# A decoder layer step on one core: the first norm's modulation weights in two column halves, and one slice of modulation weights moved out of the weight ring

## The chip, the cores and the metric

The kernel runs on one NeuronCore of a Trainium2 chip, as one program. The metric is the device time of one execution in microseconds (us). TensorE (PE) does the matrix products, VectorE (DVE), ScalarE (ACT) and GpSimd (POOL) the elementwise work; SyncE (SP), ACT and POOL issue DMA transfers.

## The reference, cut to what matters

```
mod = (silu(c) @ w_ada + b_ada).reshape(B, 1, 9, 1024)      # w_ada: 1024 x 9216
sh1, sc1, g1, sh2, sc2, g2, sh3, sc3, g3 = mod[:, :, 0..8]
h = rms_norm(x, norm_ffn1) * (1 + sc1) + sh1
x = x + 0.5 * g1 * ((silu(h @ ffn1_w_gate) * (h @ ffn1_w_up)) @ ffn1_w_down)
h = rms_norm(x, norm_mix) * (1 + sc2) + sh2
...                                   # h @ w_in; block-sparse and differential attention; w_out
x = x + g2 * mixed
h = rms_norm(x, norm_ffn2) * (1 + sc3) + sh3
x = x + 0.5 * g3 * SwiGLU_2(h)
```

There are 256 prompt tokens with one conditioning vector, and 8 sample tokens with a vector each, which read a paged cache of 1024 past positions. Model width is 1024, feed-forward width 2816. All is float32.

## The kernel before

**Layout.** Activations lie feature-major: 128 partitions times KC = 8 chunks times T = 264 tokens (256 prompt, 8 sample). Each float32 product is done as three products of rounded parts: a weight block `raw` is cut by ACT into `whi` (helper `hi`, L675) and by DVE into the rest `wlo` (helper `lo`, L973); the activations are cut likewise into `hhi` and `hlo`. `product` (L1437 to L1439) multiplies whi with hhi, whi with hlo, wlo with hhi. A weight block is 1024 x 256 values (1 MB): 8 chunks of rows times two column halves t = 0, 1, so 48 products; `hi` and `lo` cut one half of the columns at a time.

**Weight ring.** SP loads the blocks in the order of `stream_plan` into four slots `raw0` to `raw3`. A load into a slot waits until the slot's former block has been used up: for a weight block until `lo` of its second half is done, for modulation weights until PE has multiplied them. `whi` and `wlo` have two buffers each, so `hi` of half t of block n waits for the products of that half of block n-2 (`s_gemm`).

**Modulation.** The 9 x 1024 columns of `w_ada` are worked in five parts of 2048 columns (`sc` = 0 to 4, the last one of 1024), each as four pairs of row blocks: `ada(sc, q, key)` (L1464) multiplies one pair (2 MB, 8 products of 512 columns, L1488). Part 0 holds sh1 and sc1, so it has to be complete before the first norm can be applied: pairs 0 and 1 go through the ring, pairs 2 and 3 into the `early` buffers, all of them ahead of the first weight block. Parts 1 and 2 are interleaved with the first feed-forward's pairs of blocks i = 0 to 7, one ring pair each. Of part 3, pairs 0 and 1 lie outside the ring (`held_ada`, loaded by POOL when the first feed-forward's up and gate products are done) and pairs 2 and 3 go through the ring behind block W_QK; all four are multiplied by PE between the down projection and the q/k projection, in `down(..., with_ada=True)`. `mod_add` (L976) transposes a part's result and adds the bias.

**The first norm.** PE transposes x (`x_turn`, L1510), DVE copies it out of PSUM (L1074), ACT squares it (L680), PE sums the squares (`norm_sum`, L1496), ACT takes the root (L685), DVE the reciprocal (L993). After `mod_add(0)` and `coefficients` DVE and ACT make hhi and hlo chunk by chunk (`norm_rows`, L1002 and L1020; `norm_hi`, L704). Gate block 0 is multiplied chunk by chunk behind them (`block_both`), up block 0 as a whole.

**A feed-forward turn** i: gate block (banks 0, 1) and up block (banks 2, 3); ACT applies Silu to the gate banks (`silu`, L710), DVE multiplies (`act_mul`), ACT and DVE cut the result (`act_hi`, `act_lo`). The next gate block waits for `s_sil`, the next up block for `s_act`. The down projection has 12 blocks (W_DN1 = 22 on), then come W_QK (34) to 37, then key, value and gate blocks among the cache's streaming: 32 uses of 2 MB each, half loaded by SP (kvA) and half by POOL (kvB), three slots each. Semaphore thresholds fix the order of all of it by hand; every engine runs its own list in order.

## Time and profile before

| | |
|---|---|
| three runs | 788.3, 791.13, 791.59 us; median 791.13 us |
| profiled execution | 791.1 us, of it 789.4 us span |
| PE busy | 733.2 us, 93% of the span |
| DVE, ACT, POOL busy | 480.1, 320.8, 121.6 us |
| HBM read and written | 205.3 and 3.2 MB, 264 GB/s over the span |

The profile lists matmuls as they go through the array: a float32 product of this size appears as two instructions for the modulation products and the sums of squares, as one for the three cut products. Times are from the span's start. "x16" is a merged run of 16 instructions; the bracket behind a row is the engine's idle time before it and what ended it.

### The profile page before, as it was taken

How to read it: one execution, taken by the hardware profiler on the slowest of the kernel's cores; microseconds unless marked ns; L12 is line 12 of the kernel's file. 1: busy time of each engine (PE TensorE's matmuls, PEld its weight loads, DVE VectorE, ACT ScalarE, POOL GpSimd, SP SyncE). 2: the span in 40 equal slices, each digit the busy share in tenths (PEclk: the TensorE clock that was granted, in tenths of full speed). 3: DMA queues.
4: the chain of work that ended last, by engine and by line, in shares of the span. 5: the costliest groups of instructions: out<-in, count | busy, mean ns of one | idle time of the engine just before them, and what ended most of it. 6: DMA issues, size and time to landing. Idle time of an engine off the chain costs nothing.

```text
span 789.4 us, 16961 instructions
## 1 busy us (share of the span) xinstructions
PE 733.2 (93%) x6610; PEld 651.9 (83%) x6610; DVE 480.1 (61%) x684; ACT 320.8 (41%) x515; POOL 121.6 (15%) x175
## 2 busy tenths in 40 slices
PE   4599999999999798988868999999989999999997
PEld 2379898999998698877855666669979999999997
DVE  1635444564444699989988644677766455464451
ACT  1434343444433453423223534455445344444431
POOL 0000000001000300867873332310000000000000
PEclk9899999999999899999988999999999999999999
DMA  8979898858754993999999999996535555646530
GB/s 352 382 262 353 294 321 292 268 171 311 258 191 164 346 340 94 341 405 403 407 403 357 402 406 354 324 370 229 168 100 161 182 191 161 204 154 200 158 111 28
DMA packets 116521, 209.53 MB, mean 265 GB/s; under 512 B 6715, under 2 KB 100187, under 8 KB 104163
## 3 DMA queue, kind: packets, MB, share of 16 engines
q1 hardware_dynamic: 107360, 163.66, 59.7%
q0 software_dynamic: 8864, 44.82, 14.8%
q8 instruction: 46, 0.75, 0.4%
q14 instruction: 25, 0.20, 0.1%
q10 hardware_dynamic: 226, 0.10, 0.0%
HBM read 205.31 MB, written 3.24 MB: 264 GB/s over the span
## 4 chain that ended last, share of the span: by engine, by line
PE 72%; DVE 13%; DMA 9%; issue 2%; ACT 2%; SPq 1%; ACTq 0%; DVEq 0%
PE bank L1437 19%; PE bank L1438 19%; PE bank L1439 19%; DMA early<-in_w_ada 3%; PE bank L1793 3%; PE bank L1488 2%; DMA kvA<-in_cache_k_moba 2%; DMA kvA_lent<-in_cache_k_moba 2%; DVE kvA L1156 2%; DVE kvB L1156 1%; PE bank L1753 1%; DMA raw<-in_w_in 1%; PE bank L1682 1%; DVE wlo L973 1%; PE bank L1754 1%
## 5 line engine op out<-in xcount | busy, mean ns | idle before, releaser
L973 DVE TENSOR_TENSOR wlo<-raw,whi 128x1024 fp32r<-128x1024 f32 (+1 forms) x177 | 209.0, 1200 | 194.7 <-ACT whi L675 191.9
L1437 PE MATMUL bank<-hhi,whi 128*128 128x264 f32 x992 | 290.5, 293 | 15.0 <-DVE wlo L973 11.1
L1438 PE MATMUL bank<-hlo,whi 128*128 128x264 f32 x992 | 285.3, 288 | 0.0
L1439 PE MATMUL bank<-hhi,wlo 128*128 128x264 f32 x992 | 284.9, 287 | 0.0
L675 ACT ACTIVATE whi<-raw 128x1024 fp32r<-128x1024 f32 (+1 forms) x192 | 194.9, 1035 | 126.1 <-PE bank L1439 86.4
L1437 PEld LDWEIGHTS bank<-hhi,whi 128*128 128x128 f32 x992 | 191.1, 193 | 28.4 <-issue 19.1
L1438 PEld LDWEIGHTS bank<-hlo,whi 128*128 128x128 f32 x992 | 191.2, 193 | 0.2
L1439 PEld LDWEIGHTS bank<-hhi,wlo 128*128 128x128 f32 x992 | 190.2, 192 | 0.0
L1437 PE MATMUL bank<-ahi,whi 128*128 128x264 f32 x416 | 119.6, 288 | 0.4 <-DVE alo L1395 0.4
L1439 PE MATMUL bank<-ahi,wlo 128*128 128x264 f32 x416 | 118.1, 284 | 0.0
L1438 PE MATMUL bank<-alo,whi 128*128 128x264 f32 x416 | 117.8, 283 | 0.0
L1437 PEld LDWEIGHTS bank<-ahi,whi 128*128 128x128 f32 x416 | 78.2, 188 | 0.9 <-DVE alo L1395 0.6
L1438 PEld LDWEIGHTS bank<-alo,whi 128*128 128x128 f32 x416 | 78.3, 188 | 0.2
L1439 PEld LDWEIGHTS bank<-ahi,wlo 128*128 128x128 f32 x416 | 78.4, 188 | 0.0
L444 POOL DMA_DIRECT2D kvB<-in_cache_k_diff x44 | 23.2, 528 | 120.7 <-issue 66.5
L710 ACT ACTIVATE sil<-bank 128x528 f32<-128x528 f32 x22 | 13.4, 611 | 61.6 <-PE bank L1439 61.6
L714 ACT ACTIVATE ahi<-act 128x528 f32 (+1 forms) x22 | 14.2, 646 | 54.2 <-DVE act L1027 54.2
L630 POOL TENSOR_TENSOR wlo<-raw,whi 128x1024 fp32r<-128x1024 f32 x15 | 35.8, 2388 | 2.8 <-issue 2.5
L444 POOL DMA_DIRECT2D kvB<-in_cache_v_diff x44 | 23.3, 529 | 49.6 <-PE bank L1793 40.9
L1753 PE MATMUL bank<-hhi,whi 128*128 128x264 f32 x96 | 28.5, 297 | 0.0
L1031 DVE TENSOR_TENSOR alo<-act,ahi 128x528 f32 (+1 forms) x22 | 15.6, 709 | 19.2 <-ACT ahi L714 19.2
L1754 PE MATMUL bank<-hlo,whi 128*128 128x264 f32 x96 | 27.2, 284 | 0.0
(246 smaller groups left out, 803.7 us busy)
## 6 DMA issues: line engine op xcount, KB each, us to landing
raw<-in_w_ada SPq DMA_DIRECT2D x24, 1024.0 KB, 7.4
raw<-in_ffn_w_gate SPq DMA_DIRECT2D x22, 1024.0 KB, 5.5
raw<-in_ffn_w_up SPq DMA_DIRECT2D x22, 1024.0 KB, 5.3
raw<-in_w_in SPq DMA_DIRECT2D x20, 1024.0 KB, 13.1
raw<-in_ffn_w_down SPq DMA_DIRECT2D x16, 1024.0 KB, 5.2
kvB<-in_cache_k_diff POOLq DMA_DIRECT2D x44, 256.0 KB, 6.2
kvA<-in_cache_k_moba SPq DMA_DIRECT2D x44, 256.0 KB, 8.3
kvA<-in_cache_v_moba SPq DMA_DIRECT2D x44, 256.0 KB, 6.6
```

The costliest lines, as they stand in the source:

```text
L444: eng.dma_start(rows_, cache[bass.ds(page, 1)].rearrange("a (j t) d -> (a j) (t d)", t=4)).then_inc(s_kv[ab][use % KVS], 16)
L630: nc.gpsimd.tensor_tensor(half_view(wlo[n % 2], key, t), half_view(raw[s], key, t), half_view(whi[n % 2], key, t).bitcast(F32), ALU.subtra ...
L675: nc.scalar.activation(half_view(whi[key[1] % 2], key, t), half_view(raw[s], key, t), ACT.Copy).then_inc(s_hi, 1)
L973: dve.tensor_tensor(half_view(wlo[key[1] % 2], key, t), half_view(raw[s], key, t), half_view(whi[key[1] % 2], key, t).bitcast(F32), ALU.su ...
L1156: dve.transpose(slot, slot).then_inc(s_kT[ab], 1)
L1437: mm(out, wh, xh, start=start, stop=False)
L1438: mm(out, wh, xl, start=False, stop=False)
L1439: return mm(out, wl, xh, start=False, stop=stop)
L1488: ins = mm(bank[32 * j:32 * j + 32, b, 0:n].rearrange("p (t a) -> p t a", a=32), csilu[:, kc, :], cols[:, :, j, :], start=(kc == 0), stop= ...
L1753: mm(out, wh, hhi[:, k, :], start=(k == 0), stop=False)
L1754: mm(out, wh, hlo[:, k, :], start=False, stop=False)
L1793: ins = mm(bank[32 * q:32 * q + 32, 4 + ab, :], wpad[half][:, q, ab, w0:w0 + 32], kv_slot(ab, use)[:, q, :], start=(half == 0 and c % 4 == ...
```

## The change

1. **Part 0 in two column halves.** `load_first(g, q)` loads, for half g, columns 512 g to 512 g + 511 of both sh1 and sc1, for row blocks 2q and 2q+1, as two transfers of 0.5 MB into buffers of their own (`first_ada`), so part 0 leaves the ring and `early` is gone. SP's order becomes: the identity (the first 128 columns of the constants, split off POOL's transfer), x, half 0, gate block 0, up block 0, half 1, then the ring. ACT's queue has `crow` ahead of `rows`.
2. **First norm in halves.** `prescaled(g)` multiplies four chunks of x by the reciprocal root without the modulation; `mod_half(g)` transposes the half's products and adds bias and gain; `half_hi(g)` makes four chunks of hhi with one activation each (scale and bias); `half_rows(g)` makes the scaled rows and hlo.
3. **First two blocks chunk by chunk, in two passes.** PE multiplies chunks 0 to 3 of gate block 0 and up block 0 (48 products), then half 1 of part 0 (`first_products(1, q)`), then chunks 4 to 7 of both blocks. The four `s_gemm` increments come with chunk 7. POOL cuts `wlo` of gate block 0, DVE that of up block 0. PE's list at the start is reordered: the lambda product ahead of `x_turn(1)`, the sums of squares among the products of half 0.
4. **Table loads.** One-value activations (Sqrt after the exponential, Silu after the cuts of up block 0) are added.
5. **Later pairs.** Parts 1 and 2 move from turns 0 to 7 to turns 2 to 9 (`ADA_FIRST` = 2).
6. **Part 3 wholly outside the ring.** `held_ada` has eight buffers (in memory that is free at that time); POOL loads all 8 MB where it loaded four; the ring carries W_QK to W_QK + 3 right behind the down projection's blocks. POOL's clearing of `qrow` waits until part 3 is multiplied.

The diff, cut to its core (indentation reduced):

```diff
 ADA_PRO = 4
-ADA_RING = 2
+HALVES = 2
+HALF = D // HALVES
 FF_ADA = 8
+ADA_FIRST = 2
 ADA_N2 = ADA_PRO + FF_ADA


 def stream_plan():
     plan = []
     ada = lambda c: [("ada", c, 0), ("ada", c, 1)]
-    for c in range(ADA_RING):
-        plan += ada(c)
     for i in range(NPAIR):
-        plan += [("w", W_FF1 + 2 * i)] + (ada(ADA_PRO + i) if i < FF_ADA else []) + [("w", W_FF1 + 2 * i + 1)]
-    plan += [("w", W_DN1 + u) for u in range(12)] + [("w", W_QK)] + ada(ADA_N2 + 2) + ada(ADA_N2 + 3)
-    plan += [("w", n) for n in range(W_QK + 1, W_DN2 + 12)]
+        paired = ADA_FIRST <= i < ADA_FIRST + FF_ADA
+        plan += [("w", W_FF1 + 2 * i)] + (ada(ADA_PRO + i - ADA_FIRST) if paired else []) + [("w", W_FF1 + 2 * i + 1)]
...
-        held_at = [hhi_at, hlo_at, sil_at, sil_at + 4 * UNIT]
+        held_at = [hhi_at, hlo_at] + [sil_at + 4 * UNIT * e for e in range(6)]
...
+        first_ada = [[place(f"first_ada0{q}", [P, 2, 2, HALF], where=r) for q in range(KC // 2)]]
+        r = [yst_at]
+        first_ada += [[place(f"first_ada1{q}", [P, 2, 2, HALF], where=r) for q in range(KC // 2)]]
...
+    def load_first(g, q):
+
+        for k in range(2):
+            kc = 2 * q + k
+            src = A["w_ada"][0][P * kc:P * kc + P, 0:2 * D].rearrange("p (s n) -> p s n", s=2)[:, :, g * HALF:g * HALF + HALF]
+            sp.dma_start(first_ada[g][q][:, k, :, :], src).then_inc(s_first[g][q], 16)
...
+    sp.dma_start(const[:, 0:P], A["consts"][:, 0:P]).then_inc(s_ident, 16)
...
+    for q in range(KC // 2):
+        load_first(0, q)
+    load_ff(gate_w[0], 0, ("w", W_FF1))
+    load_ff(up_w[0], 0, ("w", W_FF1 + 1))
+    for q in range(KC // 2):
+        load_first(1, q)
...
-        if i < FF_ADA:
-            load_pair(ADA_PRO + i)
+        if ADA_FIRST <= i < ADA_FIRST + FF_ADA:
+            load_pair(ADA_PRO + i - ADA_FIRST)
         load_ff(up_w[0], i, ("w", W_FF1 + 2 * i + 1))
...
-    load_w(W_QK)
-    load_pair(ADA_N2 + 2)
-    load_pair(ADA_N2 + 3)
-
-    for u in range(1, 4):
+    for u in range(4):
...
+    for t in range(2):
+        lo(W_FF1, t)
...
-    for e in range(2, 4):
+    for e in range(2, 8):
...
+    nc.scalar.activation(misc[:, 20:21], misc[:, 21:22], ACT.Sqrt)
...
+    def half_hi(g):
+        for c in range(4 * g, 4 * g + 4):
+            a.wait_ge(s_mod, g + 1)
+            a.wait_ge(s_pre, c + 1)
+            nc.scalar.activation(hhi[:, c, 0:TP], work[:, c, 0:TP], ACT.Identity, bias=mod[:, c, 0:1], scale=mod[:, KC + c, 0:1]).then_inc(s_hhi, 1)
+    half_hi(0)
     hi(W_FF1, 0)
     hi(W_FF1, 1)
-    norm_hi(0, 1, KC)
     hi(W_FF1 + 1, 0)
-    ff_turn(0, W_FF1, 0, 0, 0)
-    with a.Fori(1, FF_ADA - 1) as i:
-        ff_turn(i, W_FF1, 0, 1, i - 1)
-    for i in range(FF_ADA - 1, NPAIR):
+    hi(W_FF1 + 1, 1)
+    nc.scalar.activation(misc[:, 20:21], misc[:, 21:22], ACT.Silu)
+    half_hi(1)
+    hi(W_FF1 + 2, 0)
+    hi(W_FF1 + 2, 1)
+    silu(0, W_FF1, 0)
...
+    def prescaled(g):
+        v.wait_ge(s_rstd, 1)
+        for c in range(4 * g, 4 * g + 4):
+            dve.tensor_tensor(work[:, c, 0:TP], x[:, c, 0:TP], rstd[:, 0, 0:TP], ALU.mult).then_inc(s_pre, 1)
+        ws = work[:, 4 * g:4 * g + 4, TP:T]
+        ch.link(dve.tensor_tensor(ws, x[:, 4 * g:4 * g + 4, TP:T], rstd[:, 0:1, TP:T].broadcast_to([P, 4, TS]), ALU.mult))
+    def mod_half(g):
+        v.wait_ge(s_ada, 2 * g + 2)
+        turned = adaT[:, 256 * g:256 * g + 256]
+        ch.link(dve.transpose(turned, bank[:, 4 + 3 * g, 0:256]))
+        chunks = lambda ap: ap.rearrange("p (s c) m -> p s c m", s=2)[:, :, 4 * g:4 * g + 4, :]
+        b = chunks(par[:, R_BADA:R_BADA + 2 * KC].unsqueeze(2)).broadcast_to([P, 2, 4, 9])
+        ch.link(dve.tensor_tensor(chunks(mod[:, 0:2 * KC, :]), turned.rearrange("p (s t m) -> p s t m", s=2, t=4)[:, :, :, 0:9], b, ALU.add))
+        sc = mod[:, KC + 4 * g:KC + 4 * g + 4, :]
+        gain = par[:, R_N1 + 4 * g:R_N1 + 4 * g + 4].unsqueeze(2).broadcast_to([P, 4, 9])
+        dve.scalar_tensor_tensor(out=sc, in0=sc, scalar=1.0, in1=gain, op0=ALU.add, op1=ALU.mult).then_inc(s_mod, 1)
+        v.wait_ge(s_mod, g + 1)
+    def half_rows(g):
+        c0 = 4 * g
+        four = slice(c0, c0 + 4)
+        ws = work[:, four, TP:T]
+        def row(c):
+            v.wait_ge(s_hhi, c + 1)
+            dve.tensor_scalar(work[:, c, 0:TP], work[:, c, 0:TP], mod[:, KC + c, 0:1], mod[:, c, 0:1], ALU.mult, ALU.add).then_inc(s_h, 1)
+        def low(c):
+            v.wait_ge(s_h, c + 1)
+            dve.tensor_tensor(hlo[:, c, 0:TP], work[:, c, 0:TP], hhi[:, c, 0:TP].bitcast(F32), ALU.subtract).then_inc(s_hlo, 1)
+        ch.link(dve.tensor_tensor(ws, ws, mod[:, KC + c0:KC + c0 + 4, 1:9], ALU.mult))
+        ch.link(dve.tensor_tensor(ws, ws, mod[:, four, 1:9], ALU.add))
+        ch.link(dve.tensor_copy(hhi[:, four, TP:T], ws))
+        ch.link(dve.tensor_tensor(hlo[:, four, TP:T], ws, hhi[:, four, TP:T].bitcast(F32), ALU.subtract))
+        row(c0)
+        for c in range(c0, c0 + 4):
+            if c + 1 < c0 + 4:
+                row(c + 1)
+            low(c)
...
     variance(0)
-    mod_add(0)
-    v.wait_ge(s_mod, 1)
-    coefficients(0, R_N1)
-    norm_rows(0, W_FF1)
+    prescaled(0)
+    mod_half(0)
+    half_rows(0)
+    prescaled(1)
+    v.wait_ge(s_lo, half_done(W_FF1, 1))
     lo(W_FF1 + 1, 0)
-    ff_turn(0, W_FF1, 0, 0, 0, 0)
-    with v.Fori(1, 4) as i:
-        ff_turn(i, W_FF1, 0, 0, 1, i - 1)
+    lo(W_FF1 + 1, 1)
+    mod_half(1)
+    half_rows(1)
+    lo(W_FF1 + 2, 0)
+    lo(W_FF1 + 2, 1)
+    act_mul(0, W_FF1, 0)
+    lo(W_FF1 + 3, 0)
+    act_lo(0, 0)
+    ff_turn(1, W_FF1, 0, 0, 1, 0)
...
+    def first_products(g, q):
+        pe.wait_ge(s_first[g][q], 32)
+        for k in range(2):
+            kc = 2 * q + k
+            for j in range(4):
+                cols = first_ada[g][q][:, k, :, :].rearrange("p s (t j a) -> p s t j a", j=4, a=32)[:, :, :, j, :]
+                ins = mm(bank[32 * j:32 * j + 32, 4 + 3 * g, 0:256].rearrange("p (s t a) -> p s t a", s=2, t=4), csilu[:, kc, :], cols,
+                         start=(kc == 0), stop=(kc == KC - 1))
+        if q == KC // 2 - 1:
+            ins.then_inc(s_ada, 2)
...
     x_turn(1)
-    pe.wait_ge(s_par, 2)
-    mm(bank[:, 6, 0:2], C("ones"), misc[:, 2:4], start=True, stop=True).then_inc(s_lamsum, 1)
-    ada(0, 1, 1)
+    first_products(0, 0)
     pe.wait_ge(s_lamexp, 1)
-    for cb in range(4):
-        norm_sum(0, cb)
-    ada(0, 2, None)
-    ada(0, 3, None)
+    norm_sum(0, 0)
+    norm_sum(0, 1)
+    first_products(0, 1)
+    norm_sum(0, 2)
+    norm_sum(0, 3)
+    first_products(0, 2)
+    first_products(0, 3)
+    def chunk_products(b, n, parity, t, ks):
+        for k in ks:
+            ins = product(b + t, parity, k, 256, t * P, hhi[:, k, :], hlo[:, k, :], k == 0, k == KC - 1)
+        return ins
+    early_k = KC // 2
+    pe.wait_ge(s_hlo, early_k)
+    for n in (W_FF1, W_FF1 + 1):
+        for t in range(2):
+            pe.wait_ge(s_lo, half_done(n, t))
+            chunk_products(2 * (n - W_FF1), n, n % 2, t, range(early_k))
+    for q in range(KC // 2):
+        first_products(1, q)
+    for k in range(early_k, KC):
+        pe.wait_ge(s_hlo, k + 1)
+        for n in (W_FF1, W_FF1 + 1):
+            for t in range(2):
+                ins = chunk_products(2 * (n - W_FF1), n, n % 2, t, [k])
+                if k == KC - 1:
+                    ins.then_inc(s_gemm, 1)
...
-            ada(3, 2, ADA_N2 + 2)
-            ada(3, 3, ADA_N2 + 3)
+            ada(3, 2, None)
+            ada(3, 3, None)
```

## Rows read from the trace of the kernel before

**Rows 1.** The page: GB/s moved in 40 slices of 19.7 us.
```profile
GB/s 352 382 262 353 294 321 292 268 171 311 258 191 164 346 340 94 341 405 403 407 403 357 402 406 354 324 370 229 168 100 161 182 191 161 204 154 200 158 111 28
```

**Rows 2.** Timeline of PE, 12 to 84 us: start, us, engine, line, what.
```profile
12.69 0.69 PE L1510 MATMUL bank<-const,xtok 128*128 128x128 f32 x2
...
13.51 3.64 PE L1488 MATMUL bank<-raw,csilu 128*32 128x512 f32 x16
17.09 0.44 PE L1510 MATMUL bank<-const,xtok 128*128 128x128 f32 x2
...
21.35 3.83 PE L1496 MATMUL bank<-work,const 128*128 128x264 f32 x16
...
36.93 0.56 PE L1437 MATMUL bank<-hhi,whi 128*128 128x264 f32 x1 [6.75 <-DVE wlo L973]
...
55.54 1.06 PE L1488 MATMUL bank<-raw,csilu 128*32 128x512 f32 x8 [1.80 <-DMA raw<-in_w_ada]
...
68.34 1.92 PE L1488 MATMUL bank<-raw,csilu 128*32 128x512 f32 x16
...
82.00 1.92 PE L1488 MATMUL bank<-raw,csilu 128*32 128x512 f32 x16
```

**Rows 3.** Timeline of DVE and ACT, 13 to 36 us.
```profile
13.69 1.26 DVE L1074 COPY x<-bank 128x1056 f32<-128x1056 f32 x1 [1.61 <-PE bank L1511]
...
25.79 1.80 DVE L993 RECIPROCAL rstd<-rstd 128x264 f32<-128x264 f32 x1 [4.69 <-ACT rstd L685]
...
30.25 0.72 DVE L980 STREAM_TRANSPOSE adaT<-bank 128x512 f32<-128x512 f32 x1 [2.66 <-PE bank L1488]
...
32.55 1.99 ACT L675 ACTIVATE whi<-raw 128x1024 fp32r<-128x1024 f32 x2
...
34.44 0.89 ACT L704 ACTIVATE hhi<-work,mod 128x256 fp32r<-128x256 f32 x2
```

**Rows 4.** Groups by shape: count, busy us, mean ns, idle before.
```profile
L630 POOL TENSOR_TENSOR wlo<-raw,whi 128x1024 fp32r<-128x1024 f32 x15 | 35.8, 2388 | 2.8 <-issue 2.5
...
L1002 DVE SCALAR_TENSOR_TENSOR work<-x,mod,rstd 128x256 f32<-128x256 f32 x24 | 11.6, 482 | 0.2
...
L1488 PE MATMUL bank<-last_ada,csilu 128*32 128x256 f32 x64 | 3.7, 380 | 0.0
```

**Rows 5.** Timelines of POOL and of DVE around 328 us.
```profile
327.90 2.39 POOL L630 TENSOR_TENSOR wlo<-raw,whi 128x1024 fp32r<-128x1024 f32 x1
...
327.99 2.69 DVE L1169 TENSOR_TENSOR qrow<-qrep,const 128x32 f32<-128x32 f32 x4
...
360.17 0.51 DVE L1169 TENSOR_TENSOR qrow<-qrep,const 128x32 f32<-128x32 f32 x4
```

**Rows 6.** Timelines of SP, DVE, ACT and PE, 258 to 277 us.
```profile
258.58 9.77 SPq L509 DMA_DIRECT2D raw<-in_w_in  x4
...
264.95 0.49 DVE L1020 SCALAR_TENSOR_TENSOR hlo<-work,mod,hhi 128x256 fp32r<-128x256 f32 x1 [0.25 <-ACT hhi L704]
...
268.33 2.00 ACT L675 ACTIVATE whi<-raw 128x1024 fp32r<-128x1024 f32 x2 [3.48 <-DMA raw<-in_w_in]
...
269.49 1.23 DVE L973 TENSOR_TENSOR wlo<-raw,whi 128x1024 fp32r<-128x1024 f32 x1 [4.05 <-ACT whi L675]
...
270.86 0.56 PE L1437 MATMUL bank<-hhi,whi 128*128 128x264 f32 x1 [4.38 <-DVE wlo L973]
...
276.28 1.17 PE L1646 MATMUL bank<-sqb,const 128*128 128x264 f32 x4
```

**Rows 7.** Stretches: us, busy (count) of PE, PEld, DVE, ACT, POOL; PEclk, DMA share, GB/s.
```profile
34.00:35.00 1.00, 0.00 (x0) 0.00 (x0) 1.00 (x3) 1.00 (x3) 0.00 (x0) 0.58 0.87 349
...
41.00:42.00 1.00, 1.00 (x10) 1.00 (x9) 0.68 (x2) 1.00 (x2) 0.00 (x0) 1.00 0.39 124
...
187.00:200.00 13.00, 13.00 (x109) 13.00 (x108) 6.31 (x8) 5.33 (x6) 1.05 (x2) 1.00 1.03 406
...
296.00:316.00 20.00, 17.79 (x202) 16.55 (x200) 18.27 (x20) 6.30 (x12) 1.86 (x4) 0.91 0.30 94
```

More of the change, by code:

```diff
@@ L268, in build @@
         crow = place("crow", [CROWS, P], where=r)
-        early = [place(f"early{h}", [P, UNIT], where=r) for h in range(2 * (ADA_PRO - ADA_RING))]
+        first_ada = [[place(f"first_ada0{q}", [P, 2, 2, HALF], where=r) for q in range(KC // 2)]]
+        r = [yst_at]
+        first_ada += [[place(f"first_ada1{q}", [P, 2, 2, HALF], where=r) for q in range(KC // 2)]]
         r = [region]
@@ L532, in load_pair @@
                     load_ada(c // 4, c % 4, half, ("ada", c, half))
-            for i in range(NPAIR):
+            for i in range(1, NPAIR):
                 load_ff(gate_w[0], i, ("w", W_FF1 + 2 * i))
-                if i < FF_ADA:
-                    load_pair(ADA_PRO + i)
+                if ADA_FIRST <= i < ADA_FIRST + FF_ADA:
+                    load_pair(ADA_PRO + i - ADA_FIRST)
                 load_ff(up_w[0], i, ("w", W_FF1 + 2 * i + 1))
@@ L593, in _, with lo @@
             late = CW["dist"][0]
-            pool.dma_start(const[:, 0:late], A["consts"][:, 0:late]).then_inc(s_const, 16)
+            pool.dma_start(const[:, P:late], A["consts"][:, P:late]).then_inc(s_const, 16)
+            def lo(n, t):
+                key = ("w", n)
+                s = slot_of(key)
+                pool.wait_ge(s_raw[s], landed(key))
+                pool.wait_ge(s_hi, half_done(n, t))
+                if half_done(n, t) > 1:
+                    pool.wait_ge(s_lo, half_done(n, t) - 1)
+                nc.gpsimd.tensor_tensor(half_view(wlo[n % 2], key, t), half_view(raw[s], key, t), half_view(whi[n % 2], key, t).bitcast(F32),
+                                        ALU.subtract).then_inc(s_lo, 1)
+            for t in range(2):
+                lo(W_FF1, t)
             pool.wait_ge(s_sil, 1)
@@ L734, in _ @@
             row_root(0)
-            norm_hi(0, 0, 1)
+            def half_hi(g):
[4 more added lines that the diff above has]
+            half_hi(0)
             hi(W_FF1, 0)
             hi(W_FF1, 1)
-            norm_hi(0, 1, KC)
             hi(W_FF1 + 1, 0)
-            ff_turn(0, W_FF1, 0, 0, 0)
-            with a.Fori(1, FF_ADA - 1) as i:
-                ff_turn(i, W_FF1, 0, 1, i - 1)
-            for i in range(FF_ADA - 1, NPAIR):
+            hi(W_FF1 + 1, 1)
[4 more added lines that the diff above has]
+            silu(0, W_FF1, 0)
+            hi(W_FF1 + 3, 0)
+            act_hi(0, 0)
+            ff_turn(1, W_FF1, 0, 1, 0)
+            with a.Fori(ADA_FIRST, ADA_FIRST + FF_ADA - 1) as i:
+                ff_turn(i, W_FF1, 0, ADA_FIRST, i - ADA_FIRST)
+            for i in range(ADA_FIRST + FF_ADA - 1, NPAIR):
                 ff_turn(i, W_FF1, 0, i, 0)
@@ L997, in norm_rows @@
+            def norm_rows(t):
                 v.wait_ge(s_rstd, t + 1)
@@ L1014, in norm_rows @@
                         scaled(c + 1)
-                    if weights is not None and c == 1:
-                        lo(weights, 0)
-                        lo(weights, 1)
                     v.wait_ge(s_h, KC * t + c + 1)
@@ L1467, in ada @@
                 narrow = sc == ADAS - 1
-                if q == 0 and sc >= 2:
-                    pe.wait_ge(s_adaT, sc - 1)
+                if q == 0 and sc == 2:
+                    pe.wait_ge(s_mod, 1)
+                elif q == 0 and sc > 2:
+                    pe.wait_ge(s_adaT, sc - 2)
                 for half in range(2):
                     if key_c is None:
-                        e = 2 * (q - (ADA_RING if sc == 0 else 0)) + half
-                        landing, buf = ((s_early, early) if sc == 0 else (s_last, last_ada) if narrow else (s_held, held_ada))
+                        e = 2 * q + half
+                        landing, buf = (s_last, last_ada) if narrow else (s_held, held_ada)
                         pe.wait_ge(landing[e], 16)
@@ L1543, in ff_up @@
                     block_half(2, n, 1, t, hhi, hlo)
-            for i in range(NPAIR):
-                c = ADA_PRO + i
-                if 0 < i < FF_ADA:
+            for i in range(1, NPAIR):
+                c = ADA_PRO + i - ADA_FIRST
+                if ADA_FIRST <= i < ADA_FIRST + FF_ADA:
                     ada(c // 4, c % 4, c)
-                ff_gate(i, W_FF1 + 2 * i, 0, None if i else (s_hlo, lambda k: k + 1))
-                if i == 0:
-                    ada(c // 4, c % 4, c)
+                ff_gate(i, W_FF1 + 2 * i, 0)
                 ff_up(i, W_FF1 + 2 * i + 1, 0)
```

60 lines of the change are left out of this document (26 added, 34 removed).

## The prediction, written before the result was known

> **What bounds the kernel now.** I read the slices first. TensorE is busy for 93% of the span, so elsewhere than in a few places a cheaper DMA, ACT or DVE step is worth nothing; transfers run at 340 to 405 GB/s from slice 17 on (335 us), where the cache is streamed, after a slice of only 94 GB/s [rows 1]. The change touches two places, and I read the timeline of each engine there.
>
> At the start PE does its first weight product at 36.9 us [rows 2]. The chain of waits shows why: the last `early` buffer lands at 29.1 us and is multiplied until 30.2 us, then DVE turns it (30.25 us), scales a row, ACT makes a chunk of hhi and cuts block 0 (32.55 us, two halves in 1.99), DVE cuts wlo [rows 3]. PE is idle for 6.75 us and comes back at half clock: the granted clock is 0.58 in 34 to 35 us, full again in 41 to 42 us [rows 7], after 4.1 us of products. Later PE waits 1.80 us for modulation weights (55.54 us) and starts gate block 1 right behind them, at 56.6 us. From there on it is busy; a turn with a modulation pair lasts 82.00 - 68.34 = 13.66 us, of it 1.92 the pair [rows 2].
>
> The second place is the q/k projection. W_QK + 1 is issued only at 258.58 us, because its slot still holds modulation weights that PE has to multiply; ACT cuts it at 268.33 us after 3.48 us of waiting for the transfer, DVE at 269.49, and PE starts at 270.86 us after 4.38 us idle, again at half clock, until about 276.3 us [rows 6].
>
> **Part 3 outside the ring.** With no modulation weights behind it, the ring takes W_QK + 1 to + 3 as soon as the down projection's blocks are cut, around 250 us. What ends last is then no transfer. ACT makes its last hhi by 264.85 us (DVE takes it up at 264.95 [rows 6]), cuts a half in 1.0 us (1.99 for two [rows 3]) by 265.9, DVE, free since 265.44, cuts wlo in 1.23 us, and PE starts at 267.3 us instead of 270.9: 3.6 us. It is idle for under 1 us, so the clock stays full. The 24 products that took 276.28 - 270.86 = 5.4 us at half clock take 24 x 0.121 = 2.9 us; 0.121 is a turn without its pair, 11.7 us, over 96 products [rows 2]. That is 2.5 us more, and part 3 yields 6.1 us. DVE's `mod_add(3)` (1 us) and its cuts stay ahead of PE. What is late next is DVE's own list in the q/k turns, which moves up equally, as its first member waited for the same transfers. Does the gain last? In 296 to 316 us the transfers run at 94 GB/s and 0.30 share [rows 7]: all three cache slots are full and wait for the keys to be turned, so the streaming stage starts from the same state, only earlier. Bounds: 4.8 us if PE finds the clock lowered for half of that block, 7 us if the earlier weights also spare a wait in the streaming stage. I take 6.1. Its price: 4 MB more are fetched from 187 us on, where the DMA share is 1.03 already for 13 us [rows 7]; at 0.4 MB/us they need 10 us more. A down block is consumed in 5.8 us and loaded about three blocks ahead, 15 us or more, so I take nothing; uncovered it would be 1 to 3 us.
>
> **The start.** Half 0 is 4 MB and the two blocks 2 MB; at 0.42 MB/us (352 and 382 GB/s in the first slices contain the start-up [rows 1]) half 0 lands near 19 us, the blocks by 24, half 1 by 34. No later step waits for them, as follows. What remains is a chain through four engines, and I add it up.
>
> (a) The sum of squares. The first half of x is turned by 13.6 us and copied by 14.95 [rows 3]. PE has nothing but the small lambda product in between, then turns the second half. At half clock that takes 3.4 us (pairs of 0.69 against 0.44 [rows 2]), to 18.4. Before the change the rise came at about 17 us, with 3.6 us of modulation products (16 in 3.64) behind it; now products begin only at 18.4, so I put the rise at 22.2. Quarter 0 of half 0 takes 1.8 us at half clock and 0.93 at full (64 instructions for 3.7 us in the last part, of the same shape [rows 4]); the sums take 3.83 us at full clock [rows 2]. To 20.2 the quarter, two sums to 23.1, a quarter to 24.0, two sums to 25.9. Before it was 25.2. If full clock comes at 15 us already, it is 22.8.
>
> (b) To the first product. Root and reciprocal end 2.4 us after the sum (25.2 to 27.6 [rows 3]): 28.3. `prescaled(0)` is four rows on DVE, each between 0.31 (a quarter of the 1.23 us cut [rows 6]) and 0.48 us [rows 4], with a small one: 1.5, so 29.8. `mod_half(0)`: half of the 0.72 turn and two small steps, 0.9: 30.7. ACT makes four chunks at 0.445 (two in 0.89 [rows 3]) and cuts a half of block 0: 33.6. POOL cuts its wlo in 2.39 us, where DVE took 1.23 [rows 4, 6]: 36.0. Here the engines get in each other's way: four DVE operations with two operands in SBUF take 2.69 us beside a POOL cut of 2.39, and 0.51 without one [rows 5]. DVE is still making hlo for chunks 2 and 3 when POOL begins, so the last hlo comes after POOL's first cut. I add 0.6: PE starts at 36.6 us, hardly before 36.9. The Trainium skill, page "SBUF — State Buffer", section "SBUF: two separate sides", says that such a DVE operation and a GpSimd operation exclude each other for a whole instruction; the trace agrees. With no exclusion the sum would be 0.6 here and 1 us below smaller.
>
> (c) The first pass. `prescaled(1)` is held until POOL's second cut ends at 39.2, then takes 1.5, and DVE's two cuts of up block 0 end at 41.9 and 43.1. PE, at half clock for its first 4.1 us, follows them: 48 products end at 44.8.
>
> (d) The second pass. Half 1 takes 3.7 us, to 48.5, where earlier nothing stood in front of up block 0. Then comes a wait that the change adds: `mod_half(1)` 0.9, four small steps on DVE 0.9, two rows and one low part 1.0: PE idle for 2.9 us, to 51.4. Behind it in PE's list stands everything. 48 products at full clock: 57.25.
>
> (e) A second new wait. All `s_gemm` increments come with chunk 7, so ACT may cut gate block 1 only from 56.35 on: 1.0 + 1.0, then Silu 0.6, on which the gate banks wait: PE starts gate block 1 at 59.0 instead of 56.6.
>
> (f) At that point the old kernel had done two modulation pairs of parts 1 and 2 that are still to come now: 2 x 1.93 = 3.9 us. From here on turns are the same.
>
> So the start loses 2.4 + 3.9 = 6.3 us. It counts in full, as PE runs without a pause from there to the down projection. Bounds: with full clock at 15 us (3.1 less) and no exclusion it is 2.6; if the clock also falls in the wait of (d), 4.1 us at half clock cost 2.0 more: 8.3. Splitting POOL's constants, the swap on ACT's queue and the table loads I cost at nothing: the first transposes wait for `crow` or `rows` either way, and the loads lie in ACT's waits; uncovered each is 1.3 us or less.
>
> **Sum.** -6.1 + 6.3 = +0.2 us on the profiled execution of 791.1 us (span 789.4 and 1.7 around it), which agrees with the median of 791.13. Because bound (a) can only make it smaller, I name 791.0 us.
>
> **Rivals.** (1) The start is cheap: the clock rises early and the exclusion costs little, 2.6 us lost, 791.1 - 6.1 + 2.6 = 787.6; a little less, and it is below 787.1. For it: PE did work from 10 us on in both kernels. Against it: until 17 us it did so at half clock. (2) The clock falls again in the 2.9 us wait: +2.0, 793.3. The old trace lost it in gaps of 4.4 and 6.75 us and kept it through 1.8 [rows 2, 6]; 2.9 lies between. (3) POOL's second cut gets the port before DVE's last low part, so that PE waits for that as well: +2.4, 793.6. By the same page, whoever starts first keeps the ports for the instruction, which allows this order. (4) The other side: part 3's gain is lost in the cache streaming, because that stage is paced by transfers of 64 MB at 0.4 MB/us, whenever it starts. It decides if the first cache loads do not start earlier with PE. Then only the loss stays: 791.1 + 6.3 = 797.4. Against it stands the near-idle stretch at 296 to 316 us [rows 7].
>
> **How the numbers follow.** My forecast 0.50 (own range 789 to 793), rival 1 0.27, rival 2 0.09, rival 3 0.06, rival 4 0.08. A measurement of this kernel tells 0.5%, 4 us, from no change. Below 787.1: two thirds of rival 1, 0.18. Above 795.1: rival 4 and the upper ends of 2 and 3 together, 0.14. The range reaches from rival 1 with the larger gain of part 3 to both added waits, 786.5 to 795.5.
>
> **What would show it.** In the new profile: the sum of squares ends at 25.9 us; first product at 36.6; an idle stretch of about 2.9 us in front of chunk 4 near 48.5 us; gate block 1 near 59; no wait for a transfer before W_QK + 1, and a gap of under 1 us there at full clock; the streaming stage with the same length as before. The prediction is wrong if half 0 is not complete by 24 us, if the first pass starts near 33 us, or if the streaming stage ends no earlier than q/k does relative to before.

## The result, and the profile after

The changed kernel takes 793.76 us (median of 16 runs) where the kernel before takes 790.77 (16 runs beside it): the ratio is 1.0039, with a 95% interval of 1.0023 to 1.0055, so +3.1 us (1.8 to 4.3). One of the 16 runs took 2481 us and is left out of the ratio and of all means. I had forecast 791.0, no measurable change by my bound of 0.5%. The time lies in my wide range (786.5 to 795.5) but outside the 789 to 793 that I gave to my own forecast, and the interval excludes no change: it is a small loss. A second set of 12 runs gave 1.0016 (0.9991 to 1.0041). All runs together, those of the sections below included: mean 793.1 (28 runs) against 790.6 (79 runs), +2.5 us. The profiled execution after has a span of 791.5 us against 789.4, +2.1.

PE's first instruction, before and after (timelines of PE; start us, us, engine, line, what, idle before and who ended it):

```profile
9.94 0.42 PE L1503 MATMUL bank<-const,rows 112*128 112x112 f32 x1 [9.94 <-DMA crow<-in_c_rows]
```

```profile
6.94 0.42 PE L1596 MATMUL bank<-const,rows 112*128 112x112 f32 x1 [6.94 <-DMA rows<-in_params]
```

The start, in the timelines of PE, POOL and DVE after the change:

```profile
16.13 1.94 PE L1580 MATMUL bank<-first_ada,csilu 128*32 128x256 f32 x16
18.00 2.46 PE L1589 MATMUL bank<-work,const 128*128 128x264 f32 x8
...
21.39 2.05 PE L1589 MATMUL bank<-work,const 128*128 128x264 f32 x8
...
35.78 0.56 PE L1516 MATMUL bank<-hhi,whi 128*128 128x264 f32 x1 [10.48 <-POOL wlo L608]
...
43.38 3.66 PE L1580 MATMUL bank<-first_ada,csilu 128*32 128x256 f32 x64
50.11 0.59 PE L1516 MATMUL bank<-hhi,whi 128*128 128x264 f32 x1 [3.06 <-DVE hlo L1056]
...
59.07 0.39 PE L1516 MATMUL bank<-hhi,whi 128*128 128x264 f32 x1 [1.57 <-ACT sil L718]
```

```profile
31.62 4.02 POOL L608 TENSOR_TENSOR wlo<-raw,whi 128x1024 fp32r<-128x1024 f32 x1 [29.52 <-ACT whi L683]
35.80 2.37 POOL L608 TENSOR_TENSOR wlo<-raw,whi 128x1024 fp32r<-128x1024 f32 x1 [0.17 <-POOL wlo L608]
```

```profile
27.24 0.18 DVE L1029 TENSOR_TENSOR work<-x,rstd 128x32 f32<-128x32 f32 x1
...
31.98 1.42 DVE L1027 TENSOR_TENSOR work<-x,rstd 128x256 f32<-128x256 f32 x4
33.32 2.37 DVE L1029 TENSOR_TENSOR work<-x,rstd 128x32 f32<-128x32 f32 x1
38.26 2.36 DVE L997 TENSOR_TENSOR wlo<-raw,whi 128x1024 fp32r<-128x1024 f32 x2 [2.57 <-POOL wlo L608]
```

The stretches behind it (us; busy and count of PE, PEld, DVE, ACT, POOL; granted clock; DMA share; GB/s):

```profile
36.00:39.00 3.00, 3.00 (x15) 3.00 (x16) 0.74 (x1) 0.00 (x0) 2.17 (x1) 0.50 1.10 349
...
47.00:50.00 3.00, 0.04 (x4) 0.00 (x0) 2.65 (x11) 1.91 (x4) 0.00 (x0) 0.93 0.01 5
50.00:53.00 3.00, 2.89 (x13) 2.90 (x14) 1.71 (x6) 0.16 (x1) 0.00 (x0) 0.50 0.01 3
```

There are four things to see. PE starts 3.0 us earlier, because what it waits for lands earlier: the small identity on SP's queue and `crow` at the head of ACT's. The first weight product comes at 35.78 us, 1.15 us before that of [rows 2], but it waits for POOL's cut of 4.02 us, beside which DVE does the rows of `prescaled(1)` (31.98 and 33.32). At 47 us PE stands still until the last wait of half 1 is over, and it comes back at half clock (0.50): 13 products in 2.9 us, where 25 fit at full clock. And the wait of 1.57 us for `sil` is new.

The q/k blocks, timelines of SP and PE:

```profile
249.45 6.66 SPq L514 DMA_DIRECT2D raw<-in_w_in  x2
...
273.91 0.36 PE L1516 MATMUL bank<-hhi,whi 128*128 128x264 f32 x1 [0.79 <-DVE wlo L997]
276.89 1.05 PE L1761 MATMUL bank<-sqb,const 128*128 128x264 f32 x4
```

Against [rows 6]: no wait for a transfer, 0.79 us idle instead of 4.38, and 3.0 us for the half block instead of 5.4.

**Where the 2.1 us of the two profiles are.** I use four marks that both kernels have: the pair of x updates that follows a wait of 2.81 us near the end of the first down projection (DVE, 258.53 after, 251.90 before), the first turn of keys (DVE), and the extraction of the samples' columns in column groups 3 and 7 (PE, 16 instructions, 4 columns wide). Behind each time stands the distance to the mark before.

```
                x update   first key turn   group 3           group 7          end of span
before           251.90    296.50 (44.60)   477.74 (181.24)   525.13 (47.39)   789.4 (264.3)
after            258.53    296.98 (38.45)   476.53 (179.55)   526.58 (50.05)   791.5 (264.9)
lag              +6.63     +0.48            -1.21             +1.45            +2.1
```

The start costs 6.63 us (forecast 6.3), part 3 gives 6.15 (forecast 6.1). The rest, +1.6 (2.1 less the 0.48 of the first key turn), arises behind the first key turn, where not one instruction differs; it first gains 1.7 and then loses 3.3. There the stretches of the changed kernel show the clock at half twice:

```profile
477.00:480.00 3.00, 3.00 (x29) 1.78 (x29) 2.30 (x3) 1.54 (x2) 0.00 (x0) 0.94 0.95 380
480.00:483.00 3.00, 3.00 (x14) 2.27 (x11) 1.83 (x9) 0.00 (x0) 1.12 (x3) 0.50 0.80 270
...
525.00:528.00 3.00, 3.00 (x14) 2.73 (x12) 2.42 (x3) 1.17 (x3) 0.61 (x1) 0.50 0.74 290
528.00:531.00 3.00, 3.00 (x13) 2.57 (x13) 1.51 (x4) 2.10 (x5) 0.81 (x2) 0.50 0.73 216
```

and those of the kernel before once, and shorter:

```profile
480.00:483.00 3.00, 3.00 (x28) 1.81 (x21) 2.89 (x10) 0.00 (x0) 0.54 (x2) 1.00 0.65 240
...
525.00:528.00 3.00, 2.65 (x21) 2.19 (x19) 2.96 (x4) 2.55 (x4) 1.44 (x3) 1.00 1.00 334
528.00:531.00 3.00, 2.39 (x12) 2.39 (x13) 2.71 (x5) 2.87 (x5) 0.71 (x2) 0.68 0.99 367
```

### The profile page after: what moved, and what is told of

It reads as the page before. It is cut to its first block, busy times and chain, and to the rows that moved or that the text cites. A ratio compares the mean times of both kernels' runs of the same rounds, so it can differ in the third digit from the quotient of the medians.

```text
span 791.5 us, 17132 instructions
## 1 busy us (share of the span) xinstructions
PE 734.4 (93%) x6674; PEld 653.5 (83%) x6674; DVE 482.2 (61%) x698; ACT 321.1 (41%) x517; POOL 130.2 (16%) x181
## 4 chain that ended last, share of the span: by engine, by line
PE 75%; DVE 14%; DMA 4%; issue 2%; ACT 2%; SPq 1%; POOL 1%; ACTq 0%; DVEq 0%; POOLq 0%
PE bank L1516 20%; PE bank L1517 19%; PE bank L1518 19%; DMA kvA<-in_cache_k_moba 4%; PE bank L1908 3%; PE bank L1569 2%; DVE kvA L1235 2%; DVE kvB L1235 1%; PE bank L1868 1%; PE bank L1589 1%; PE bank L1869 1%; PE bank L1870 1%; DVE rstd L1215 1%; DVE wlo L997 1%; PE bank L1797 1%
## 5 line engine op out<-in xcount | busy, mean ns | idle before, releaser
L997 DVE TENSOR_TENSOR wlo<-raw,whi 128x1024 fp32r<-128x1024 f32 (+1 forms) x175 | 206.2, 1199 | 192.8 <-ACT whi L683 187.5
L1518 PE MATMUL bank<-hhi,wlo 128*128 128x264 f32 x992 | 282.8, 285 | 0.0
L1516 PEld LDWEIGHTS bank<-hhi,whi 128*128 128x128 f32 x992 | 189.0, 191 | 32.2 <-issue 25.8
L1517 PEld LDWEIGHTS bank<-hlo,whi 128*128 128x128 f32 x992 | 189.1, 191 | 0.2
L1518 PEld LDWEIGHTS bank<-hhi,wlo 128*128 128x128 f32 x992 | 188.1, 190 | 0.0
L608 POOL TENSOR_TENSOR wlo<-raw,whi 128x1024 fp32r<-128x1024 f32 x17 | 42.2, 2483 | 33.1 <-ACT whi L683 29.5
L1870 PE MATMUL bank<-hhi,wlo 128*128 128x264 f32 x96 | 27.6, 287 | 0.0
```

Source lines behind the costliest of these rows:

```text
L608: nc.gpsimd.tensor_tensor(half_view(wlo[n % 2], key, t), half_view(raw[s], key, t), half_view(whi[n % 2], key, t).bitcast(F32), ALU.subtra ...
L997: dve.tensor_tensor(half_view(wlo[key[1] % 2], key, t), half_view(raw[s], key, t), half_view(whi[key[1] % 2], key, t).bitcast(F32), ALU.su ...
L1516: mm(out, wh, xh, start=start, stop=False)
L1517: mm(out, wh, xl, start=False, stop=False)
L1518: return mm(out, wl, xh, start=False, stop=stop)
L1870: ins = mm(out, wl, hhi[:, k, :], start=False, stop=(k == KC - 1))
```

## The experiments

### Each part alone, and the changed kernel again

Part 3 alone, on the kernel before (its edit cut to the core; plan, semaphores and POOL's wait as in the change):

```diff
-held_at = [hhi_at, hlo_at, sil_at, sil_at + 4 * UNIT]
+held_at = [hhi_at, hlo_at] + [sil_at + 4 * UNIT * e for e in range(6)]
...
-            load_w(W_QK)
-            load_pair(ADA_N2 + 2)
-            load_pair(ADA_N2 + 3)
-            for u in range(1, 4):
+            for u in range(4):
                 load_w(W_QK + u)
```

> The kernel before with part 3's two ring pairs moved to buffers outside the ring, and its start as it was. Theory A (the lead that part 3 gains is kept to the start of the cache stream and about half of it is given back behind it, where the matrix engine's clock falls in the branch stage): the QK+1 block starts some 6 us earlier than before, the time is 786.5 to 788 (-3 to -4.5). Theory B (part 3's gain is kept whole, and what the changed kernel loses beyond my sum comes with its start): -6.1, about 784.7. Rival (the streams of the caches set the end of part 3 anyway): 789 to 791.

Measured: 785.76 us, ratio 0.9927 (0.9900 to 0.9953), -5.8 us (-7.9 to -3.7). The rival is out; theory B's -6.1 is nearer than A's, though the interval reaches into A's. In its trace no clock fall that before does not have comes behind part 3 (marks below).

The start alone, on the changed kernel, with the same lines the other way round:

> The changed kernel with part 3 put back into the ring as before, so only the start is changed. Theory A (the start costs what the first down-projection shows, 6.6 us): +6.6, about 797.4. Theory B (the start also shifts something behind it, a clock fall or a transfer in the streaming stage, for some 2 to 3 us more): +9 to +10, about 800. Rival (the caches' stream catches up with a late start): +3 or less.

Measured: 799.66 us, ratio 1.0098 (1.0065 to 1.0130), +7.8 us (5.1 to 10.3). The rival is out; the time does not tell A from B, but the marks do for this trace: 7.1 us at the end of the first down projection, and some 2 more in the cache streaming. The two single runs add up to -5.8 + 7.8 = +2.0 us, which agrees with the +2.5 of both parts together: nothing in the times asks for an interaction of the two.

The changed kernel, unchanged:

> The changed kernel once more, unchanged. If the clock fall around 522 to 537 us belongs to this kernel, its profile shows again half the clock there and a lag against the kernel before that steps from about +0.4 to about +2.1 us; if it was chance, the lag stays near +0.5 and the fall is elsewhere or as in the kernel before. Time 1.0039 of the kernel before (793.8) if the earlier ratio stands, 1.0006 (791.3) if only the two mechanisms of my sum count.

Measured: 792.65 us, ratio as given above; its interval holds both expected values, 1.0039 and 1.0006. Its trace has the fall at 480 us again, but not the long one at 525:

```profile
525.00:528.00 3.00, 2.42 (x15) 1.69 (x13) 2.00 (x4) 0.58 (x2) 0.00 (x0) 1.00 1.09 373
528.00:531.00 3.00, 2.22 (x16) 1.76 (x16) 2.71 (x4) 2.78 (x6) 1.86 (x3) 1.00 0.80 251
531.00:534.00 3.00, 2.82 (x16) 2.82 (x17) 2.97 (x5) 2.97 (x4) 0.28 (x1) 0.68 0.97 363
```

### More traces of the same kernels

> The kernel before once more, unchanged, for a second trace. If the clock falls of the streaming stage are a matter of chance, they and their lengths differ from those of the first trace, as the changed kernel's did between its two traces. If the fall near 480 us, which all three traces with both the new start and the new part 3 show, belongs to these, it is absent here again.

> The kernel before once more, unchanged, for a third trace: the end of the first down-projection within +0 to +1 us of the first trace, and no fall near 480 us, if that belongs to the kernels with both parts.

> The changed kernel once more, unchanged, for a third trace: first down-projection's end 6 to 7.6 us behind the first trace of the kernel before, and, if the fall near 480 us belongs to the kernels with both parts, it is there again, 1.6 us long in its effect; if it is absent, it is a matter of how often.

> Part 3's edit alone once more, for a second trace. Theory (its lead of 6.2 us does not depend on the start, and the streaming stage takes or gives back 1 to 3 us by where the clock falls): the QK+1 block's lead is 6.2 us again, and the later steps of the lag differ from those of its first trace.

One execution each, at 788.92, 787.49, 792.72 and 785.46 us. The same marks in all traces of these four kernels:

```
                x update   first key turn   group 3           group 7          end of span
before, 2nd      252.93    296.47 (43.54)   475.57 (179.10)   522.98 (47.41)   787.2 (264.2)
before, 3rd      252.16    295.25 (43.09)   472.53 (177.28)   521.58 (49.05)   785.8 (264.2)
after, 2nd       259.53    297.98 (38.45)   478.67 (180.69)   527.71 (49.04)   791.9 (264.2)
after, 3rd       258.73    297.17 (38.44)   477.83 (180.66)   526.86 (49.03)   791.0 (264.2)
part 3 alone     252.20    290.64 (38.44)   471.29 (180.65)   518.69 (47.40)   782.9 (264.2)
  2nd trace      251.89    290.34 (38.45)   472.19 (181.85)   519.58 (47.39)   783.8 (264.2)
start alone      258.97    303.86 (44.89)   486.99 (183.13)   534.40 (47.41)   798.7 (264.3)
```

Four things follow. With the old start the first mark is at 252.2 us in the mean of five traces (251.89 to 252.93), with the new one at 259.2 in five (258.53 to 260.25, that of the fill below among them, whose edit comes later): the start costs 7.0 us. From there to the first key turn the kernels with part 3 outside the ring take 38.44 to 38.47 us in all ten traces, but those with it in the ring 43.09 to 44.89, mean 44.0: part 3 gives 5.6 us on average, and 6.15 only against the trace that I had. W_QK + 1 starts 19.0, 18.2, 17.8 and 18.4 us behind the x update in the four traces with the ring, 15.4 in the others, so of the 5.6 us the stall itself is 3.0 on average. Its half block took 5.4, 4.5, 4.5 and 4.3 us against 3.0, which is 1.7 more, and 0.9 comes behind it. Part of the difference is the clock behind the stall. The first trace of before and its second, in the stretches at 270 us:

```profile
270.00:273.00 3.00, 2.14 (x10) 2.17 (x11) 2.79 (x4) 0.76 (x2) 0.20 (x1) 0.50 1.06 401
273.00:276.00 3.00, 3.00 (x15) 3.00 (x15) 1.54 (x2) 2.58 (x4) 0.00 (x0) 0.50 1.06 357
```

```profile
270.00:273.00 3.00, 1.86 (x8) 1.89 (x9) 2.96 (x4) 1.99 (x3) 1.23 (x2) 0.69 1.09 383
273.00:276.00 3.00, 3.00 (x20) 2.97 (x19) 2.46 (x3) 1.62 (x3) 0.00 (x0) 0.74 1.03 371
```

Third, between the first key turn and group 3 the 14 traces of this document take 177.3 to 183.1 us. Part of this goes with the clock: summed over 18 equal stretches, the granted clock stood at half for 10.2 us in three of them (177.3, 179.6 and 179.6 us long) and for 17 to 24 us in the other eleven (179.1 to 183.1). Fourth, from group 3 on a trace takes 47.4 + 264.2 = 311.6 us, or 1.6 us more where the clock falls near 480 us, or 3.4 more where the long fall near 525 comes on top (the trace with the fill apart). The fall near 480 was in all three traces of the changed kernel, in one of three of the kernel before, in none of part 3 alone (two) and of the start alone (one). So my expectation that before would never show it is refuted: it is a matter of how often. The second trace of part 3 has its first key turn 6.2 us ahead of the first trace of before, as expected.

### A fill for the clock

```diff
                 if c % 4 == 3:
+                    for _f in range(6):
+                        mm(bank[:, 6, 384:512], C("ones"), ident, start=True, stop=True)
                     pe.wait_ge(s_om, c // 4 + 1)
```

> The changed kernel with six extra matrix products (all ones by the identity, into a bank that nobody reads) behind the output products of column groups 3 and 7, where the engine waits 0.5 us for the gates and then makes products only 4 columns wide; the clock fell right behind these in the changed kernel's traces (at 480 and, in one, at 523). Their work is estimated at 1.3 us each time, 0.5 of it in the wait. Theory (the low work of this place lets the clock fall there, 1.6 us each time that it does): no fall near 480, and the time 0 to -1.5 against the changed kernel. Rival (the fall has its cause further back, or the fill is too little): the fall stays, and the time is +1 to +1.6.

Measured: 794.17 us, ratio 1.0052 (1.0032 to 1.0072); its mean is 1.3 us above the changed kernel's, so the theory's gain did not come. The clock stayed up near 480, as the theory said, but fell near 526, ahead of the second fill (its instructions start at 528.90):

```profile
482.00:485.00 3.00, 3.00 (x26) 1.55 (x27) 2.89 (x10) 0.00 (x0) 0.04 (x1) 1.00 0.62 238
...
523.00:526.00 3.00, 3.00 (x15) 0.65 (x7) 0.88 (x3) 0.00 (x0) 0.73 (x1) 1.00 1.06 372
526.00:529.00 3.00, 2.42 (x8) 2.03 (x8) 1.98 (x4) 0.49 (x1) 0.00 (x0) 0.57 1.08 371
```

```profile
526.61 1.22 PE L1891 MATMUL bank<-osq,const 128*128 128x256 f32 x2 [0.58 <-ACT pts L933]
...
528.90 1.95 PE L1961 MATMUL bank<-const 128*128 128x128 f32 x12
530.68 1.85 PE L1966 MATMUL bank<-const,om 128*128 128x4 f32 x16
```

The changed kernel's first trace is alike there: granted clock 0.52 in 524 to 525 us, the narrow products only at 526.58. So at group 7 neither the narrow products nor the wait that the fill covers can be what the clock fell for, as the expectation had it. Its marks of groups 3 and 7 are 480.48 and 530.68, 50.2 us apart, no less than with a fall. The rival's time came true, by another way. One trace does not show that the fill kept the clock up; it shows that buying it this way does not pay.

### Undoing what the new start lost

DVE cuts the first block, GpSimd nothing there:

```diff
 # VectorE
             half_rows(0)
+            lo(W_FF1, 0)
+            lo(W_FF1, 1)
             prescaled(1)
-            v.wait_ge(s_lo, half_done(W_FF1, 1))
 # GpSimd
-            for t in range(2):
-                lo(W_FF1, t)
```

> The changed kernel with the first weight block's low parts cut by VectorE right behind the first half's rows (two cuts of about 1 us in the traces) instead of by GpSimd. GpSimd's first cut took 4.02 us beside VectorE's row products where an undisturbed one takes 2.4. Theory (the first product waits for GpSimd's cut): first product at about 33.4 to 34 instead of 35.8 after the same start of the sums, and the first down-projection 2 to 2.7 us earlier, so about 2.4 us below the changed kernel. Rival (the first pass runs into another wait, the second block's low parts on VectorE or the second half's weights, and gives it back): 0 to -0.5.

Measured: 790.64 us, ratio 1.0000 (0.9978 to 1.0021), 2.5 us below the changed kernel's mean (means of all runs, 790.7 and 793.1).

```profile
33.61 0.56 PE L1515 MATMUL bank<-hhi,whi 128*128 128x264 f32 x1 [8.04 <-DVE wlo L995]
49.05 0.39 PE L1515 MATMUL bank<-hhi,whi 128*128 128x264 f32 x1 [3.07 <-DVE hlo L1054]
58.22 0.39 PE L1515 MATMUL bank<-hhi,whi 128*128 128x264 f32 x1 [1.57 <-ACT sil L716]
```

Counted from ACT's root (23.74 here, 23.48 after) the first product is 2.4 us earlier, the second pass only 1.3 and gate block 1 only 1.1. The clock took the rest: it is 0.50 until past 39 us here as there, so PE had it for 2.5 us longer:

```profile
36.00:39.00 3.00, 3.00 (x15) 3.00 (x15) 2.40 (x3) 0.08 (x1) 0.00 (x0) 0.50 1.09 347
39.00:42.00 3.00, 3.00 (x25) 3.00 (x24) 0.00 (x0) 0.00 (x0) 0.00 (x0) 0.88 1.10 348
```

Other traces of the changed start have the first product at the same 12.3 us behind the root, but gate block 1 and the x update up to 0.9 us later than its first trace. Against their mean the x update, 233.9 us behind the root here, is 1.5 us earlier (235.1 to 236.0 in five). So the start gives about 1.5 us, and of the 2.5 measured the rest fits its late part without a fall near 480 (47.40 between groups 3 and 7).

The second pass by blocks:

```diff
-            for k in range(early_k, KC):
-                pe.wait_ge(s_hlo, k + 1)
-                for n in (W_FF1, W_FF1 + 1):
-                    for t in range(2):
+            for n in (W_FF1, W_FF1 + 1):
+                for t in range(2):
+                    for k in range(early_k, KC):
+                        pe.wait_ge(s_hlo, k + 1)
                         ins = chunk_products(2 * (n - W_FF1), n, n % 2, t, [k])
```

> The changed kernel with its second pass in the order of the weight blocks instead of chunk by chunk over both: the first block's products are done one block's products earlier, so ScalarE can cut the next weights and do the Silu under the second block's. Theory: the wait of 1.57 us ahead of the second gate block goes, -1.6. Rival (the second pass then waits for the last chunk's rows, about 1 us behind its start, for as much): 0 to -0.5.

Measured: 792.01 us, ratio 1.0015 (0.9993 to 1.0037), 0.8 below the changed kernel's mean. In the trace no wait is left between the second pass (51.85 us) and the turns, and the x update comes 233.9 us after the root instead of 235.1 to 236.0: 1.5 us on average, near the theory's 1.6. The runs' 0.8 lies between theory and rival.

The second half's modulation products ahead of the first pass:

```diff
+            for q in range(KC // 2):
+                first_products(1, q)
             early_k = KC // 2
             pe.wait_ge(s_hlo, early_k)
             ...
-            for q in range(KC // 2):
-                first_products(1, q)
             for k in range(early_k, KC):
```

> The changed kernel with the second half's modulation products on the matrix engine ahead of the first pass instead of behind it; nothing else differs. They fill an idle stretch of 10.5 us; the last of their weights land at about 36, so the first pass starts at about 37.3 instead of 35.8, but the second pass finds its rows at about 43.7 instead of 50.1. Theory (the order of these products costs the wait of 3.1 us, the 3.7 us of products and the half clock behind them): -6.4 to -8 against the changed kernel, about 786.5. Rival (the second half's weights land much later than 36, or the rows' engine is the bound anyway): -1 to -3, about 791.

Measured: 786.34 us, ratio 0.9934 (0.9905 to 0.9962), 6.3 below the changed kernel in the same set, just short of the theory's 6.4 to 8; the rival is out.

```profile
31.14 1.15 PE L1580 MATMUL bank<-first_ada,csilu 128*32 128x256 f32 x16 [2.71 <-DMA first_ada<-in_w_ada]
33.86 1.94 PE L1580 MATMUL bank<-first_ada,csilu 128*32 128x256 f32 x16 [1.57 <-DMA first_ada<-in_w_ada]
36.58 1.93 PE L1580 MATMUL bank<-first_ada,csilu 128*32 128x256 f32 x16 [0.78 <-DMA first_ada<-in_w_ada]
...
53.60 0.39 PE L1516 MATMUL bank<-hhi,whi 128*128 128x264 f32 x1 [1.57 <-ACT sil L718]
```

The last of these weights land at 36.6 us; the products follow them as they come, there is no wait between the two passes, and gate block 1 starts 28.9 us after the root instead of 35.6, the x update 228.3 instead of 235.4 in the mean.

All of it, with the last two pieces of products between the two blocks of the first pass:

```diff
+            first_products(1, 0)
+            first_products(1, 1)
             ...
             for n in (W_FF1, W_FF1 + 1):
+                if n > W_FF1:
+                    first_products(1, 2)
+                    first_products(1, 3)
                 for t in range(2):
```

> The changed kernel with four edits: VectorE's cut of the first weight block, the second pass by blocks, the second half's modulation products ahead of the second pass (the first two pieces before the first weight block, the last two between the two blocks). If the gains add: about -6.5 to -7 for the products' order, -2.4 for the cut, -1.6 for the pass, together 9 to 11 us below the changed kernel, about 783. Rival (the landing of the second half's weights at 34 to 37 us and the rows of VectorE now bound the start, so that the cut and the pass bring nothing on top): as with the products' order alone, 786 to 787.

Measured: 784.18 us, ratio 0.9902 (0.9869 to 0.9935), by the ratio 7.7 us below the kernel before (5.1 to 10.4; 6.9 by the means of all runs) and 9.4 below the changed one's mean. The gains of the three edits (6.6, 2.5 and 0.8 by the same means, 9.9 in sum) add to within 0.5 us, and the rival's 786 to 787 is out:

```profile
31.25 1.93 PE L1579 MATMUL bank<-first_ada,csilu 128*32 128x256 f32 x16 [1.63 <-DMA first_ada<-in_w_ada]
33.84 0.56 PE L1515 MATMUL bank<-hhi,whi 128*128 128x264 f32 x1 [0.67 <-DVE wlo L995]
...
249.10 0.88 DVE L1117 SCALAR_TENSOR_TENSOR x<-bank,mod,x 128x256 f32<-128x256 f32 x2 [2.81 <-PE bank L1517]
```

The last wait of the start is this one of 0.67 us at 33.84, and the x update stands at 249.10, 3.1 us ahead of the old start's mean. It is the best version found, and the only form of the new start that beats the old one. Its late part has both falls (50.06 and 264.9), so the gain is not the clock's.

## Why the prediction was wrong, step by step

**Part 3** was right in mechanism. In my trace W_QK + 1 starts 273.91 - 258.53 = 15.4 us behind the x update, where it was 270.86 - 251.90 = 19.0: 3.6 us, as forecast. The rest is full clock, and the gain was not eaten by the cache streaming: 38.45 us stand in all traces, and part 3 alone measured -5.8. Rival 4 is refuted. Both terms were read from the trace with the longest stall and the longest half clock of the three of before: on average over four traces the stall is worth 3.0 instead of 3.6 and all behind it 2.6 instead of 2.5, in sum 5.6. Of these 2.6 the half block gives 1.7, the rest comes after it.

One reading was loose, without an effect on the sum: transfers run at 324 to 407 GB/s from slice 17 to slice 27 only (316 to 533 us), and at 229 or less behind it.

**The start**, term by term. (a) The sum of squares ended at 23.5 us, not 25.9. The first products began at 16.1 instead of 18.4, and here a term failed that I had put at nothing: the split of the constants and the swap on ACT's queue. The first transposes did wait for `rows`, but it landed 3.0 us before `crow` had (6.94 against 9.94), and DVE's first copy of x came at 11.54 instead of 13.69. Then only the first quarter and some of the first sums were slow (1.94 us against 1.07 for the same 16 instructions). I call that half clock from these times alone, here as in the prediction: the profile's granted clock reads 1.00 from 8 to 24 us after the change and from 8 to 18 us before it. This is most of rival 1's condition, but (b) took it back: POOL's first cut lasted 4.02 us instead of 2.39, because it and DVE's operations with two operands in SBUF kept each other waiting. The row at 33.32 shows the other side, a DVE step of 0.18 us that took 2.37. The first product came at 35.78, forecast 36.6. The Trainium skill, page "SBUF — State Buffer", section "SBUF: two separate sides", has these two exclude each other for a whole instruction; both rows agree, and I had priced it at 0.6 us where it cost 1.6. What stood in POOL's way was `prescaled(1)`: I had held it until POOL's second cut ends at 39.2, but DVE did it at 31.98. Rival 3 did not come: the last low part was made before POOL's first cut ended. (c) 43.4 us instead of 44.8, as `prescaled(1)` was out of the way and DVE's two cuts ended at 40.6 instead of 43.1. (d) The wait was 3.06 us, forecast 2.9, but rival 2, to which I had given 0.09, came true: behind the wait the clock was at half, in all three traces (50 to 53 us here). The second pass, "48 products at full clock", took 7.4 us instead of 5.85, and gave back the lead of 1.3 us. (e) The wait of 1.57 us stood where I had put it, and gate block 1 started at 59.07, forecast 59.0. (f) Two pairs to come: 6.63 - (59.07 - 56.6) = 4.2 us, forecast 3.9. The sum was +6.63 against 6.3 in this trace, 7.0 in the mean. So that this total was nearly right is luck: (a) and (b), (c) and (d) were wrong in opposite directions. Rival 2's number, 793.3, is near the 793.1 of all runs, but that is luck in part too: what (a) and (c) gained, part 3 and the stages behind it lost again.

**The steps that failed** are three. First, in (d), "48 products at full clock": the clock did not last through the wait that the change adds, and from the first product to the x update the new start takes 223.1 us in the mean of five traces, the old one 215.4, so 7.7 more where my terms make 22.4 - 19.7 + 3.9 = 6.6. (Its first product comes 0.7 us earlier in the same means.) Second, the unspoken step that the kernel before's single trace stands for its mean, which sized part 3 at 6.1 where it is 5.6. These make the sum 7.0 - 5.6 = +1.4 instead of +0.2. Third, "the streaming stage with the same length as before". Behind the first key turn, from group 3 to the end, traces differ by 0, 1.6 or 3.4 us by where the clock falls. The changed kernel had the fall near 480 us, worth 1.6 us, in three traces of three, and so had three of the four variants with both parts and no fill (mod_early, by_block, combined; not dve_cut); the kernels with one part or none had it in one of six. That would explain the missing 1.1 us of the measured 2.5. It is argued from counts, not shown: no run moved this fall alone, since the trace in which the fill took it away has another. The stretch before it is as good a candidate: from the first key turn to group 3 the three traces after take 180.3 us in the mean, those before 179.2, in a scatter that goes in part with the time at half clock. Nor do the runs' mean granted clocks tell: 0.9755 in the 28 runs after, 0.9760 in 63 before. And the missing 1.1 is itself not clear of noise: the +2.5 of all runs is sure to 0.8 us, the +1.4 of the traces to 1.1, estimated from their scatter. Whether the changed kernel loses time behind the first key turn, and why it should, stays open.

## What to carry to other kernels

Before work is split to start earlier, ask what the engine that matters does in the idle stretch that stays: here 32 modulation products (64 instructions) waited behind the first pass although PE was idle for 10.5 us ahead of it, and moving four calls turned a loss of 2.5 us into a gain of 4 to 5. Do not give a cut to GpSimd beside a VectorE that is busy with two-operand steps in SBUF and is itself next on the path. And where a forecast of well under 1% rests on one trace, take its stalls at half clock as one draw: their price varied by 1.8 us in a place where no instruction changed.
